# The last gate group in two halves: 256 columns in each of two banks

## The chip, the cores and the metric

The kernel runs on one core of one Trainium2 chip. The metric is the device time of one execution, in microseconds (us). TensorE multiplies and writes into PSUM, ScalarE (ACT) and VectorE (DVE) work on PSUM and SBUF, GpSimd (POOL) has no part in the end of this kernel, and SyncE (SP) issues the transfers.

## What is computed

One layer of a decoder trunk on x of 512 rows and 1024 columns, in float32: a mixer, a feed-forward part, and then the gate, followed by a last normalization. Only the last two matter here:

```python
h = h + (hid * hid) @ w_ff2[i]
gate = jax.nn.sigmoid(rmsnorm(h, ple_norm_g[i]) @ w_ple_gate[i])
h = h + gate * (p[i] @ w_ple_proj[i])
return rmsnorm(h, final_norm_g)
```

with rmsnorm(x, g) = x * rsqrt(mean(x * x) + 1e-6) * g, the mean taken over a row of 1024 columns.

## The kernel before

Every matrix product is done with operands that are split in two parts (a high part and the rest), both float32r: three matmuls of 512 columns stand for one product (`product`, lines 1120 to 1124: high by high, high by low, low by high). Rows go in four groups of 128 (s = 0 to 3). A block of weights b has 512 columns. PSUM has four banks `acc`, one for each row group, and four banks `side` for transposes.

The gate product comes last. It has two blocks, GATE and GATE + 1 (columns 0 to 511 and 512 to 1023), and so eight groups i = 0 to 7, with b = GATE + i // 4 and s = i % 4. For each, TensorE runs `group_rows` (line 1126): eight steps over k, each with the three matmuls of `product`, 24 matmuls of 512 columns into bank s of `acc`. The stationary operand is the normalized, transposed h (`b_hi`, `b_lo`), the moving one the weights (`w_hi`, `w_lo`). The last matmul of a group raises `acc_full`.

The order on each engine is written out by hand and strict. Engines meet only at semaphores. For each group ScalarE (lines 708 to 741) takes the sigmoid from the bank into `conv` (line 719), then in block GATE + 1 runs a square root of one column (line 722), whose only use is that the table of the square root is loaded at this point, then squares h with a row sum (line 727), and then: for a group of block GATE adds eps in an Identity (line 731, `f_base`), for a group of block GATE + 1 takes the square root over both halves of the row (line 735, `f_rms`). VectorE (lines 1075 to 1099) multiplies the gate into y, which holds p @ w_ple (line 1085, raises `gated`), adds it to h (line 1087, raises `h_final`, on which ScalarE's square waits), multiplies h by the gain of the last norm (line 1091, `h_gain`), and for block GATE + 1 takes the reciprocal (line 1094) and scales the whole row (line 1098). For the last group alone VectorE scales the first 640 columns and ScalarE the other 384 (line 740). SyncE sends each row group out as soon as it is scaled (line 355), and the program ends when the four transfers have landed.

A sigmoid and a square root are in different tables of ScalarE, so each group of block GATE + 1 has two ACT_TABLE_LOAD in the profile: one before its sigmoid (line 719), which runs as soon as the group before is finished, and one before the one-column square root (line 722). Square, Identity and Copy run with either.

Of the kernel before, what the change touches and what calls it, by code (L numbers as in the profile page):

```python
# [5 lines left out]
P = 128  # L6
F32 = mybir.dt.float32
F32R = mybir.dt.float32r
ALU = mybir.AluOpType
ACT = mybir.ActivationFunctionType  # L10
# [4 lines left out]
V, X, BC, U, Z, OUT, PLE, FF, GATE = 0, 2, 4, 5, 7, 9, 13, 14, 30  # L15
EPS = 1e-6
WARM = 10
OUT_DVE = 640


def build_layer(nc, a, out):


    _, SEQ, D = a["x"].shape
    NS = SEQ // P
    KT = D // P
# [22 lines left out]
    with ExitStack() as ctx:  # L49
        def sb(name, shape, dt=F32, where=ctx):  # L50
            return where.enter_context(nc.sbuf_tensor(name, shape, dt))
# [6 lines left out]
        w_hi = sb("w_hi", [P, 2, 8, 512], F32R)  # L58
        w_lo = sb("w_lo", [P, 2, 8, 512], F32R)
        a_hi = sb("a_hi", [P, KT, SEQ], F32R)  # L60
        a_lo = sb("a_lo", [P, KT, SEQ], F32R)
        h = sb("h", [P, NS, D])
        y = sb("y", [P, NS, D])
# [8 lines left out]
        cols = sb("cols", [P, 68])  # L72
# [7 lines left out]
        cs = sb("cs", [P, NS * R])  # L80
        csT = sb("csT", [NS * R, P])
        decay = sb("decay", [P, 3, NS, R])
        f_ssq = sb("f_ssq", [P, 8])
        f_base = sb("f_base", [P, NS])
        f_rms = sb("f_rms", [P, NS])
        f_rstd = sb("f_rstd", [P, NS])
        ssq = sb("ssq", [P, 12])
# [9 lines left out]
        with ExitStack() as early:  # L97
            conv = sb("conv", [P, 2, 512], where=early)
            xs_t = sb("xs_t", [P, 2, 512], where=early)
# [19 lines left out]
        b_hi = sb("b_hi", [P, KT, SEQ], F32R)  # L119
        b_lo = sb("b_lo", [P, KT, SEQ], F32R)  # L120


        acc = ctx.enter_context(nc.psum_tensor("acc", [P, 4, 512], F32))
# [8 lines left out]
        acc_full = sem("acc_full")  # L132
        act_evac = sem("act_evac")
# [34 lines left out]
        gated, h_final, h_gain = sem("gated"), sem("h_final"), sem("h_gain")  # L168
        f_ssq_ready, f_base_ready, f_rms_ready = sem("f_ssq_ready"), sem("f_base_ready"), sem("f_rms_ready")
# [21 lines left out]
        def emptied(b, s, shift=0):  # L191


            return (act_evac if kind[b].endswith("act") else dve_evac), before[b] + s + 1 + shift
# [228 lines left out]
        def _(act):  # L423
# [105 lines left out]
            for t in range(4 * OUT):  # L529
                b, s = divmod(t, 4)  # L530
# [14 lines left out]
                if 10 <= t < 18:  # L545
                    bank = wait_full(act, ("xs", t - 10))
                    if t == 10:
                        wait_free(act, ("ws", 1))
                    ins = act.activation(y[:, :, (t - 10) * P:(t - 10) * P + P],
                                         bank.rearrange("p (c n) -> p c n", c=NS), ACT.Copy)  # L550
                    freed(ins, ("xs", t - 10))
                if t == 11:
                    bank = wait_full(act, "dt")
                    act.wait_ge(small_landed, 16 * 4)
                    ins = act.activation(dtT[:], bank[0:2 * R, :], ACT.Identity, bias=dt_b[:])
# [5 lines left out]
                if t == 16:  # L561
                    bank = wait_full(act, "decay")
                    act.wait_ge(cs_ready, 1)
                    ins = act.activation(decay[:].rearrange("p a c r -> p (a c r)"), bank[:, 0:3 * NS * R], ACT.Exp)
                    freed(ins, "decay")
                if 16 <= t < 20:
                    for i in range(2):
                        head = 2 * (t - 16) + i
                        bank = wait_full(act, ("mix", head))
# [3 lines left out]
                if 19 <= t < 21:  # L573
                    g = t - 19
                    bank = wait_full(act, ("b_nat", g))
                    ins = act.activation(b_nat[:, g].rearrange("p c n -> p (c n)"), bank, ACT.Copy)
# [128 lines left out]
                sums(2, s)  # L705


            for i in range(8):
                b, s = GATE + i // 4, i % 4
                if i == 0:  # L710
                    xt_evac(2, 2)
                if i == 2:
                    xt_evac(2, 3)
                if b == GATE:
                    split_hi(GATE + 1, s)
                act.wait_ge(acc_full, 4 * b + s + 1)
                if i >= 2:
                    act.wait_ge(gated, i - 1)
                act.activation(conv[:, i % 2, :], acc[:, s, :], ACT.Sigmoid).then_inc(act_evac, 1)
                if b > GATE:  # L720
                    act.wait_ge(sqrt_loaded, s + 1)
                    act.activation(early_rms[:], eps[:], ACT.Sqrt).then_inc(sqrt_loaded, 1)

                act.wait_ge(h_final, i + 1)
                if i:
                    act.wait_ge(f_ssq_ready, i)
                act.activation(xs_t[:, 0, :], h[:, s, 512 * (i // 4):512 * (i // 4) + 512], ACT.Square,
                               accum_out=f_ssq[:, i:i + 1]).then_inc(f_ssq_ready, 1)
                act.wait_ge(f_ssq_ready, i + 1)
                if b == GATE:  # L730
                    act.activation(f_base[:, s:s + 1], f_ssq[:, i:i + 1], ACT.Identity, bias=eps[:], scale=1.0 / D
                                   ).then_inc(f_base_ready, 1)
                else:
                    act.wait_ge(f_base_ready, s + 1)
                    act.activation(f_rms[:, s:s + 1], f_ssq[:, i:i + 1], ACT.Sqrt, bias=f_base[:, s:s + 1],
                                   scale=1.0 / D).then_inc(f_rms_ready, 1)
                if i == 7:
                    act.wait_ge(f_rstd_ready, s + 1)
                    act.wait_ge(h_gain, 4 + s + 1)
                    act.activation(y[:, s, OUT_DVE:], y[:, s, OUT_DVE:], ACT.Copy, scale=f_rstd[:, s:s + 1]  # L740
                                   ).then_inc(out_act, 1)

# [2 lines left out]
        def _(dve):  # L745
# [326 lines left out]
                normed(2, s)  # L1072


            for i in range(8):
                b, s = GATE + i // 4, i % 4
                if i == 0:
                    xt_evac(2, 2)
                if i == 2:
                    xt_evac(2, 3)  # L1080
                if b == GATE:
                    split_lo(GATE + 1, s)
                at = slice(512 * (i // 4), 512 * (i // 4) + 512)
                dve.wait_ge(*emptied(b, s))
                dve.tensor_tensor(y[:, s, at], y[:, s, at], conv[:, i % 2, :], ALU.mult).then_inc(gated, 1)
                dve.wait_ge(gated, i + 1)
                dve.tensor_tensor(h[:, s, at], h[:, s, at], y[:, s, at], ALU.add).then_inc(h_final, 1)
                dve.wait_ge(h_final, i + 1)
                if i == 0:
                    dve.wait_ge(gain_landed[0], 16 * 4)  # L1090
                dve.tensor_tensor(y[:, s, at], h[:, s, at], gain[:, 0, at], ALU.mult).then_inc(h_gain, 1)
                if b > GATE:
                    dve.wait_ge(f_rms_ready, s + 1)
                    dve.reciprocal(f_rstd[:, s:s + 1], f_rms[:, s:s + 1]).then_inc(f_rstd_ready, 1)
                    dve.wait_ge(f_rstd_ready, s + 1)
                    dve.wait_ge(h_gain, i + 1)
                    end = OUT_DVE if i == 7 else D
                    dve.tensor_scalar(y[:, s, 0:end], y[:, s, 0:end], f_rstd[:, s:s + 1], None, ALU.mult
                                      ).then_inc(out_dve, 1)

# [2 lines left out]
        def _(pe):  # L1103
            def banks_free(b, s, trip=None):

                if b == 0:
                    return
                c, r = last_user(b, s)
                signal, value = emptied(c, r)
                pe.wait_ge(signal, value if trip is None else value + 8 * trip)  # L1110
                if trip is not None and b == FF + 1:


                    signal, value = emptied(FF + 4, 2 + s // 2)
                    pe.wait_ge(signal, value - 8 + 8 * trip)
# [4 lines left out]
            def product(dst, st, mv, start, stop):  # L1120

                pe.matmul(dst, st[0], mv[0], start=start, stop=False)  # L1122
                pe.matmul(dst, st[0], mv[1], start=False, stop=False)  # L1123
                return pe.matmul(dst, st[1], mv[0], start=False, stop=stop)  # L1124

            def group_rows(b, s, act_hl, between=None):


                banks_free(b, s)
                for k in range(KT):  # L1130
                    if between and k == KT - 2:
                        between()
                    if b == 0 and k % 4 == 0:
                        wait_free(pe, ("xt", 0, s, k // 4))
                    if s == 0 and k % 2 == 0:
                        split_ready(b, k // 2)
                    at = (slice(None), k, slice(s * P, s * P + P))
                    ins = product(acc[:, s, :], [t[at] for t in act_hl],
                                  [t[:, b % 2, k, :] for t in (w_hi, w_lo)], k == 0, k == KT - 1)
                ins.then_inc(acc_full, 1)  # L1140

            def group_cols(b, s, act_hl, trip=None):
# [215 lines left out]
            for i in range(8):  # L1358
                b, s = GATE + i // 4, i % 4
                if b == GATE:  # L1360
                    for q in range(2):
                        wait_free(pe, ("xt", 2, s, q))
                group_rows(b, s, B)
                if i == 1:
                    turn_norm(2, 3)

# [22 lines left out]
```

## Time and profile before

| | |
|---|---|
| time, median of 3 runs | 778.98 us (777.57, 778.98, 779.05) |
| span of the profiled execution | 775.9 us |
| time of the profiled execution | not recorded apart from its span |
| median less span | 3.1 us |
| TensorE busy | 763.0 us, 98% of the span |
| VectorE busy | 436.4 us, 56% |
| ScalarE busy | 326.1 us, 42% |
| mean granted clock of TensorE | 0.997 |

The span runs from the first to the last instruction of one execution; the time is that of executions without the profiler. A busy engine isn't an engine at its peak. The chain of work that ended last is followed back from the last instruction to what released each step. In a row of the timeline the columns are start, duration, engine, line, operation, tiles and shapes (partitions x elements), and in brackets how long the engine sat idle before and what ended this. "PE" is TensorE's matmul and "PEld" its loading of weights. The end of a matmul is modelled, and so the distance between the starts of two matmuls says more than their duration.

### The profile page before, as it was taken

Reading aid. Unit: us, or ns where it says so; the run is one execution under the profiler, and the core shown is the slowest. Engines: PE = TensorE matmul, PEld = TensorE weight load, DVE = VectorE, ACT = ScalarE, POOL = GpSimd, SP = SyncE. Lnnn points to the kernel's source line nnn. Section 1 sums busy time; section 2 is a strip of 40 time slices with the busy share of each in tenths; the row PEclk is TensorE's granted clock in tenths of the full one; section 3 lists DMA queues with packets and bytes.
Section 4 is the critical chain, followed back from the end, with each engine's and each line's share of the span. In section 5 each row is a group of like instructions: output and inputs, shape, how many; then the busy total and the mean of one; then the engine's idle time right before and its main releaser. Section 6 shows DMA issues by size and latency. Waiting matters only on the chain.

```text
span 775.9 us, 9090 instructions
## 1 busy us (share of the span) xinstructions
PE 763.0 (98%) x3492; PEld 623.3 (80%) x3492; DVE 436.4 (56%) x488; ACT 326.1 (42%) x456; POOL 87.5 (11%) x60
## 2 busy tenths in 40 slices
PE   8999999999999999999999999999999999999996
PEld 7888877888887888888888888888888888888885
DVE  5556884668579575457445353444444444446754
ACT  6525446655485823127433140413223140323556
POOL 1022210864652000000000000000000000000000
PEclk9999999999999999999999999999999999999998
DMA  8622333333323443123323233232323233232102
GB/s 333 187 82 82 108 98 115 116 108 103 143 82 103 166 139 110 44 76 124 109 85 106 87 103 108 81 108 81 108 81 108 81 102 97 92 122 82 48 0 109
DMA packets 35193, 81.88 MB, mean 106 GB/s; under 512 B 3924, under 2 KB 5592, under 8 KB 35160
## 3 DMA queue, kind: packets, MB, share of 16 engines
q1 hardware_dynamic: 33928, 77.20, 30.5%
q10 hardware_dynamic: 1232, 4.23, 1.8%
q8 instruction: 22, 0.36, 0.2%
q14 instruction: 11, 0.09, 0.0%
HBM read 79.28 MB, written 2.13 MB: 105 GB/s over the span
## 4 chain that ended last, share of the span: by engine, by line
PE 93%; DVE 3%; ACT 1%; issue 1%; DMA 1%; SPq 0%; ACTq 0%; DVEq 0%
PE acc L1122 29%; PE acc L1124 29%; PE acc L1123 29%; PE side L1184 3%; PE side L1277 2%; DVE w_lo L751 1%; PE side L1244 1%; DVE conv L948 1%; DMA gain<-in_norm_mix_g 1%; PE side L1284 1%; PE side L1272 1%; DVE h L937 0%; PE acc L1201 0%; ACT w_hi L431 0%; PE side L1224 0%
## 5 line engine op out<-in xcount | busy, mean ns | idle before, releaser
L1122 PE MATMUL acc<-w_hi,a_hi 128*128 128x512 f32 x512 | 204.2, 399 | 0.0
L1124 PE MATMUL acc<-w_hi,a_lo 128*128 128x512 f32 x512 | 199.5, 390 | 0.0
L1123 PE MATMUL acc<-w_lo,a_hi 128*128 128x512 f32 x512 | 199.4, 390 | 0.0
L431 ACT ACTIVATE w_hi<-w_raw 128x1024 fp32r<-128x1024 f32 (+1 forms) x128 | 130.1, 1036 | 145.9 <-PE acc L1124 143.6
L751 DVE TENSOR_TENSOR w_lo<-w_raw,w_hi 128x1024 fp32r<-128x1024 f32 (+1 forms) x128 | 166.1, 1299 | 45.0 <-ACT w_hi L431 44.3
L802 DVE TENSOR_TENSOR h<-h,acc 128x1024 f32<-128x1024 f32 x48 | 58.6, 1221 | 106.5 <-PE acc L1124 106.5
L1122 PEld LDWEIGHTS acc<-w_hi,a_hi 128*128 128x128 f32 x512 | 96.2, 188 | 21.0 <-issue 1.4
L1123 PEld LDWEIGHTS acc<-w_lo,a_hi 128*128 128x128 f32 x512 | 96.2, 188 | 20.6 <-issue 1.4
L1124 PEld LDWEIGHTS acc<-w_hi,a_lo 128*128 128x128 f32 x512 | 96.1, 188 | 20.3
L1124 PE MATMUL acc<-b_hi,w_lo 128*128 128x512 f32 x256 | 100.9, 394 | 0.0
L1122 PE MATMUL acc<-b_hi,w_hi 128*128 128x512 f32 x256 | 100.9, 394 | 0.0
L1123 PE MATMUL acc<-b_lo,w_hi 128*128 128x512 f32 x256 | 100.9, 394 | 0.0
L1048 DVE TENSOR_TENSOR tmp<-tmp 128x512 f32<-128x512 f32 x32 | 22.2, 693 | 76.5 <-ACT tmp L487 76.5
L487 ACT ACTIVATE tmp<-acc 128x512 f32<-128x512 f32 x32 | 19.1, 598 | 96.8 <-PE acc L1124 96.8
L1122 PEld LDWEIGHTS acc<-b_hi,w_hi 128*128 128x128 f32 x256 | 47.9, 187 | 11.9
L1124 PEld LDWEIGHTS acc<-b_hi,w_lo 128*128 128x128 f32 x256 | 47.9, 187 | 11.8
L1123 PEld LDWEIGHTS acc<-b_lo,w_hi 128*128 128x128 f32 x256 | 47.9, 187 | 11.8
L1122 PE MATMUL acc<-w_hi,b_hi 128*128 128x512 f32 x128 | 50.8, 397 | 0.0
L1124 PE MATMUL acc<-w_hi,b_lo 128*128 128x512 f32 x128 | 50.2, 392 | 0.0
L1123 PE MATMUL acc<-w_lo,b_hi 128*128 128x512 f32 x128 | 49.8, 389 | 0.0
L1122 PE MATMUL acc<-a_hi,w_hi 128*128 128x512 f32 x96 | 38.9, 405 | 0.0
L1124 PE MATMUL acc<-a_hi,w_lo 128*128 128x512 f32 x96 | 37.5, 390 | 0.0
(183 smaller groups left out, 819.1 us busy)
## 6 DMA issues: line engine op xcount, KB each, us to landing
w_raw<-in_w_ff SPq DMA_DIRECT2D x64, 512.0 KB, 3.5
w_raw<-in_w_in SPq DMA_DIRECT2D x36, 512.0 KB, 3.9
w_raw<-in_w_out SPq DMA_DIRECT2D x16, 512.0 KB, 3.4
h<-in_x SPq DMA_DIRECT2D x8, 512.0 KB, 4.4
seg<-cs_dram ACTq DMA_DIRECT2D x8, 512.0 KB, 3.8
w_raw<-in_w_ple_gate SPq DMA_DIRECT2D x8, 512.0 KB, 3.9
out<-y SPq DMA_DIRECT2D x4, 512.0 KB, 2.6
w_raw<-in_w_ple_proj SPq DMA_DIRECT2D x4, 256.0 KB, 2.6
```

The source lines that it names most:

```text
L431: act.activation(w_hi[:, half, 2 * p:2 * p + n, :], w_raw[:, p, 0:n, :], ACT.Copy).then_inc(hi_ready, 1)
L487: act.activation(tmp[:, s % 2, :], acc[:, s, :], ACT.Relu).then_inc(act_evac, 1)
L751: dve.tensor_tensor(w_lo[:, half, 2 * p:2 * p + n, :], w_raw[:, p, 0:n, :], w_hi[:, half, 2 * p:2 * p + n, :].bitcast(F32), ALU.subtract). ...
L802: dve.tensor_tensor(hs, hs, acc[:, i:i + 2, :], ALU.add).then_inc(dve_evac, 1)
L948: ins = dve.scalar_tensor_tensor(dst, acc[:, s, 0:SEQ - k], w, dst, ALU.mult, ALU.add)
L1048: dve.tensor_tensor(tmp[:, 2 + s % 2, :], tmp[:, s % 2, :], tmp[:, s % 2, :], ALU.mult).then_inc(sq_ready, 1)
L1122: pe.matmul(dst, st[0], mv[0], start=start, stop=False)
L1123: pe.matmul(dst, st[0], mv[1], start=False, stop=False)
L1124: return pe.matmul(dst, st[1], mv[0], start=False, stop=stop)
L1184: ins = pe.transpose(bank[:, i * P:i * P + P], src(i), ident[:])
L1244: filled(pe.matmul(bank.rearrange("p (c n) -> p c n", c=NS), wsT[:, g, :], h[:, :, g * P:g * P + P], start=True, stop=True), ("mix", g))
L1277: ins = pe.matmul(bank[:, r * HD:r * HD + HD], lm[:, r, :], xdt[:, r * HD:r * HD + HD], start=True, stop=True)
```

## The change

The eighth group (i = 7) becomes two, i = 7 and i = 8, with 256 columns each: 512 to 767 of the row into bank 3, 768 to 1023 into bank 0. TensorE runs eight steps over k for the first half and then eight for the second, with the same stationary tiles loaded again, so 48 matmuls of 256 columns. Before the second half it waits for the sigmoid of group 4 (i = 4), the last user of bank 0. ScalarE and VectorE do the steps of the two groups one after the other, in the same strict order, each step over 256 columns. The first half has no one-column square root; in place of the square root an Identity adds its sum of squares to `f_base` (a fifth column), and the second half's square root takes this as its bias. The reciprocal and the scaling come once, after the second half. `f_ssq` grows from 8 to 9 columns and `f_base` from 4 to 5. `emptied` is no longer asked for each group; the count that it gave for the first is counted up by i, which is the same number for i = 0 to 7.

```diff
@@ the tiles
-        f_ssq = sb("f_ssq", [P, 8])
-        f_base = sb("f_base", [P, NS])
+        f_ssq = sb("f_ssq", [P, 9])
+        f_base = sb("f_base", [P, NS + 1])
@@ ScalarE
-            for i in range(8):
-                b, s = GATE + i // 4, i % 4
+            for i in range(9):
+                b, s = (GATE + i // 4, i % 4) if i < 8 else (GATE + 1, 3)
...
-                act.wait_ge(acc_full, 4 * b + s + 1)
+                bank, n = (s, 512) if i < 7 else ((3, 256) if i == 7 else (0, 256))
+                at = slice(512 * (i // 4), 512 * (i // 4) + 512) if i < 7 else slice(512 + 256 * (i - 7), 768 + 256 * (i - 7))
+                act.wait_ge(acc_full, 4 * GATE + i + 1)
                 if i >= 2:
                     act.wait_ge(gated, i - 1)
-                act.activation(conv[:, i % 2, :], acc[:, s, :], ACT.Sigmoid).then_inc(act_evac, 1)
-                if b > GATE:
+                act.activation(conv[:, i % 2, 0:n], acc[:, bank, 0:n], ACT.Sigmoid).then_inc(act_evac, 1)
+                if b > GATE and i != 7:
                     act.wait_ge(sqrt_loaded, s + 1)
                     act.activation(early_rms[:], eps[:], ACT.Sqrt).then_inc(sqrt_loaded, 1)
 
                 act.wait_ge(h_final, i + 1)
                 if i:
                     act.wait_ge(f_ssq_ready, i)
-                act.activation(xs_t[:, 0, :], h[:, s, 512 * (i // 4):512 * (i // 4) + 512], ACT.Square,
+                act.activation(xs_t[:, 0, 0:n], h[:, s, at], ACT.Square,
                                accum_out=f_ssq[:, i:i + 1]).then_inc(f_ssq_ready, 1)
                 act.wait_ge(f_ssq_ready, i + 1)
                 if b == GATE:
                     act.activation(f_base[:, s:s + 1], f_ssq[:, i:i + 1], ACT.Identity, bias=eps[:], scale=1.0 / D
                                    ).then_inc(f_base_ready, 1)
+                elif i == 7:
+                    act.wait_ge(f_base_ready, s + 1)
+                    act.activation(f_base[:, 4:5], f_ssq[:, i:i + 1], ACT.Identity, bias=f_base[:, s:s + 1],
+                                   scale=1.0 / D).then_inc(f_base_ready, 1)
                 else:
-                    act.wait_ge(f_base_ready, s + 1)
-                    act.activation(f_rms[:, s:s + 1], f_ssq[:, i:i + 1], ACT.Sqrt, bias=f_base[:, s:s + 1],
+                    base = s if i < 7 else 4
+                    act.wait_ge(f_base_ready, base + 1)
+                    act.activation(f_rms[:, s:s + 1], f_ssq[:, i:i + 1], ACT.Sqrt, bias=f_base[:, base:base + 1],
                                    scale=1.0 / D).then_inc(f_rms_ready, 1)
-                if i == 7:
+                if i == 8:
                     act.wait_ge(f_rstd_ready, s + 1)
-                    act.wait_ge(h_gain, 4 + s + 1)
+                    act.wait_ge(h_gain, 9)
@@ VectorE
-                dve.wait_ge(*emptied(b, s))
-                dve.tensor_tensor(y[:, s, at], y[:, s, at], conv[:, i % 2, :], ALU.mult).then_inc(gated, 1)
+                dve.wait_ge(act_evac, emptied(GATE, 0)[1] + i)
+                dve.tensor_tensor(y[:, s, at], y[:, s, at], conv[:, i % 2, 0:n], ALU.mult).then_inc(gated, 1)
...
-                if b > GATE:
+                if b > GATE and i != 7:
                     dve.wait_ge(f_rms_ready, s + 1)
...
-                    end = OUT_DVE if i == 7 else D
+                    end = OUT_DVE if i == 8 else D
@@ TensorE
+            def last_half(half):
+
+                b, s, bank = GATE + 1, 3, (3, 0)[half]
+                if half == 0:
+                    banks_free(b, s)
+                else:
+                    pe.wait_ge(act_evac, emptied(b, 0)[1])
+                cols = slice(256 * half, 256 * half + 256)
+                for k in range(KT):
+                    ins = product(acc[:, bank, 0:256], [t[:, k, s * P:s * P + P] for t in (b_hi, b_lo)],
+                                  [t[:, b % 2, k, cols] for t in (w_hi, w_lo)], k == 0, k == KT - 1)
+                ins.then_inc(acc_full, 1)
...
-                group_rows(b, s, B)
+                if i < 7:
+                    group_rows(b, s, B)
+                else:
+                    for half in range(2):
+                        last_half(half)
```

## Rows read from the trace of the kernel before

**Rows 1.** The page: TensorE's share, and the chain's shares by engine.

```profile
PE 763.0 (98%) x3492; PEld 623.3 (80%) x3492; DVE 436.4 (56%) x488; ACT 326.1 (42%) x456; POOL 87.5 (11%) x60
...
PE 93%; DVE 3%; ACT 1%; issue 1%; DMA 1%; SPq 0%; ACTq 0%; DVEq 0%
```

**Rows 2.** The chain that ended last, from 765 us: start, duration, what.

```profile
768.57 0.25 PE acc L1124
...
769.45 1.28 ACT L722
```

**Rows 3.** Timeline of ScalarE, end of group 6 to the end.

```profile
766.49 1.28 ACT L719 ACT_TABLE_LOAD   x1
768.84 0.60 ACT L719 ACTIVATE conv<-acc 128x512 f32<-128x512 f32 x1 [1.06 <-PE acc L1124]
769.45 1.28 ACT L722 ACT_TABLE_LOAD   x1
770.75 0.20 ACT L722 ACTIVATE early_rms<-eps 128x1 f32<-128x1 f32 x1
770.92 0.63 ACT L727 ACTIVATE xs_t<-h 128x512 f32<-128x512 f32 x1
...
771.67 0.29 ACT L735 ACTIVATE f_rms<-f_ssq,f_base 128x1 f32<-128x1 f32 x1
772.20 0.61 ACT L740 ACTIVATE y<-y,f_rstd 128x384 f32<-128x384 f32 x1 [0.23 <-DVE f_rstd L1094]
```

**Rows 4.** Timeline of VectorE over the same stretch.

```profile
766.71 0.75 DVE L1098 TENSOR_SCALAR y<-y,f_rstd 128x1024 f32<-128x1024 f32 x1
769.47 0.69 DVE L1085 TENSOR_TENSOR y<-y,conv 128x512 f32<-128x512 f32 x1 [2.01 <-ACT conv L719]
770.19 0.69 DVE L1087 TENSOR_TENSOR h<-h,y 128x512 f32<-128x512 f32 x1
...
772.00 0.16 DVE L1094 RECIPROCAL f_rstd<-f_rms 128x1 f32<-128x1 f32 x1 [0.39 <-ACT f_rms L735]
```

**Rows 5.** Last group: first and last matmul, a load, the stretch with its granted clock.

```profile
763.14 0.39 PE L1122 MATMUL acc<-w_hi,b_hi 128*128 128x512 f32 x1
...
768.40 0.40 PE L1124 MATMUL acc<-w_hi,b_lo 128*128 128x512 f32 x1
...
763.14 0.19 PEld L1123 LDWEIGHTS acc<-w_lo,b_hi 128*128 128x128 f32 x1
...
763.14:768.60 5.46, 5.46 (x25) 4.32 (x23) 2.99 (x5) 4.36 (x7) 0.00 (x0) 1.00 0.24 97
```

**Rows 6.** Matmuls of 64 and 128 columns: durations (min/median/max), timeline, granted clock (1.00).

```profile
L1277 PEld LDWEIGHTS side<-xdt,lm x128: 187/192/192, 147.6 to 251.9; 128*128 128x128 f32 x128
L1277 PE MATMUL side<-xdt,lm x128: 218/275/275, 147.9 to 252.0; 128*128 128x64 f32 x128
...
147.87 1.89 PE L1277 MATMUL side<-xdt,lm 128*128 128x64 f32 x16
...
8.82 2.40 PE L1201 MATMUL acc<-ones,ident 128*128 128x128 f32 x20
...
147.87:149.54 1.67, 1.67 (x17) 1.67 (x15) 0.39 (x1) 1.67 (x3) 0.00 (x0) 1.00 0.26 49
```

**Rows 7.** Groups of instructions by form, 724 to 776 us, of 1024 columns.

```profile
L451 ACT ACTIVATE tmp<-h 128x1024 f32<-128x1024 f32 x1 | 1.1, 1059 | 3.1 <-DVE h L802 3.1
...
L751 DVE TENSOR_TENSOR w_lo<-w_raw,w_hi 128x1024 fp32r<-128x1024 f32 x4 | 4.9, 1222 | 2.8 <-ACT w_hi L431 2.7
```

**Rows 8.** Timeline of ScalarE, end of group 0.

```profile
732.33 0.29 ACT L731 ACTIVATE f_base<-f_ssq,eps 128x1 f32<-128x1 f32 x1
732.53 1.04 ACT L431 ACTIVATE w_hi<-w_raw 128x1024 fp32r<-128x1024 f32 x1
```

**Rows 9.** Output transfers: issues with first and last start, and landing times.

```profile
L355 SPq DMA_DIRECT2D out<-y x4: 332/344/356, 756.5 to 772.9; - x4
...
DMA to landing us min/median/max: 2.6/2.6/4.7
```

More of the change, by code:

```diff
@@ L1072, in _ @@
                 normed(2, s)
-            for i in range(8):
-                b, s = GATE + i // 4, i % 4
+            for i in range(9):
+                b, s = (GATE + i // 4, i % 4) if i < 8 else (GATE + 1, 3)
                 if i == 0:
@@ L1082, in _ @@
                     split_lo(GATE + 1, s)
-                at = slice(512 * (i // 4), 512 * (i // 4) + 512)
-                dve.wait_ge(*emptied(b, s))
-                dve.tensor_tensor(y[:, s, at], y[:, s, at], conv[:, i % 2, :], ALU.mult).then_inc(gated, 1)
+                n = 512 if i < 7 else 256
+                at = slice(512 * (i // 4), 512 * (i // 4) + 512) if i < 7 else slice(512 + 256 * (i - 7), 768 + 256 * (i - 7))
+                dve.wait_ge(act_evac, emptied(GATE, 0)[1] + i)
+                dve.tensor_tensor(y[:, s, at], y[:, s, at], conv[:, i % 2, 0:n], ALU.mult).then_inc(gated, 1)
                 dve.wait_ge(gated, i + 1)
```

## Prediction, made before the changed kernel was run

> **What bounds the kernel now.** I read three things in this order. First the busy shares and the chain's shares by engine [rows 1]: TensorE has work for 98% of the span and 93% of the chain that ended last runs through it. So for nearly all of the kernel a change has to touch TensorE's stream to be felt. Second, the end of that chain [rows 2]: it leaves TensorE with the last matmul at 768.57 us and goes on through ScalarE and VectorE. The change lives here, because its subject is the last group of matmuls, 128 rows by 512 columns of the gate product, and what must follow it before the output can be sent. Third, the tail instruction by instruction on ScalarE and VectorE [rows 3, 4]. From the start of the last sigmoid (768.84) to the start of the last output scaling (772.20) lie 3.36 us, and two chains run side by side in it:
> - ScalarE: sigmoid, 0.61 to the load of the square root's table, 1.30 to a one-column square root that only carries this load, 0.17 to the square [rows 3]. Sum 2.08.
> - VectorE: 0.63 to the gating product, 0.725 to the add into h and 0.725 until the square may start at 770.92 [rows 3, 4]. Sum 2.08.
>
> They end together. Behind them come square, read of its sum and square root (0.75 from 770.92 to 771.67), reciprocal (0.33), scaling (0.20 to its start) [rows 3, 4]. The output transfer is issued at 772.9 and lands 2.6 us later [rows 9]. The time before is 778.98 and the profiled span 775.9 (the table above), so 3.1 us lie around the span; the profiled execution has no separate time, and I take span plus 3.1 as its time, which is the median of the three runs by construction. The sum below gives a difference at 772.20, which goes unchanged into the span and the median, for the last transfer is the same size.
>
> **TensorE's part.** Removed are 24 matmuls of 512 columns, added are 48 of 256, each with its own load of 128x128 weights. The last group's matmuls start at 763.14 and 768.40, 23 intervals apart, so 0.2287 us each [rows 5]. The trace has no matmul of 256 columns. Bounds for its interval d:
> - The moving stream: half of 0.2287 is 0.114. At the upper of the two clock levels, 2.4 GHz, 512 columns take 0.213, so each matmul has 0.015 on top of its stream; 256 columns are then 0.107 + 0.015 = 0.122. The granted clock in this stretch is 1.00 [rows 5].
> - The weight load: sixteen matmuls of 64 columns, each with a load, take 1.89 us with the last one's own record of 0.275 taken off, so (1.89 - 0.275) / 15 = 0.108; twenty of 128 columns give (2.40 - 0.275) / 19 = 0.112 [rows 6]. A row of loads alone can't go faster than about 0.108, and it doesn't matter there whether 64 or 128 columns stream beside it. So load and stream lie beside each other.
> - Upper end: load and stream one behind the other, 0.108 + 0.114 = 0.222.
>
> I take 0.122, as the nearest rows (128 columns at 0.112 and 512 at 0.229, load hidden in both) lie on either side. The last matmul then starts at 763.14 + 47 x 0.122 = 768.87, 0.47 later than now. From its start to the sigmoid it is 0.44 now [rows 3, 5]; with 256 columns fewer in it 0.44 - 0.11 = 0.33. The second half is ready at 769.20 instead of 768.84. The first half is ready at 763.14 + 23 x 0.122 + 0.33 = 766.28. The second half's own wait, for bank 0, is for a sigmoid that ended over 10 us before, and costs nothing.
>
> **The 256-wide operations.** The trace has none of this width. ScalarE's square takes 1.059 us for 1024 and 0.63 for 512 columns [rows 3, 7], so 0.83 ns a column, and 256 columns fewer save 0.21. VectorE takes 1.222 for 1024 and 0.69 for 512 [rows 4, 7], 1.04 ns a column, and saves 0.265. Bounds: nothing is saved at all (ScalarE's scaling of only 384 columns took 0.61 [rows 3], no less than a sigmoid of 512), or the whole duration is halved. I take the slopes, since they come from the same engine and the same shapes of operand.
>
> **The first half.** The diff leaves ScalarE's program in strict order: sigmoid of the first half, its square, an Identity in place of the square root, and only then the sigmoid of the second half. The wait for h_final is new in this place: behind it on ScalarE stands the second sigmoid, and everything waits for that. When does the first sigmoid start? Not with its data (766.28): ScalarE finishes group 6 at 766.49 and then loads the sigmoid's table, as now, 1.30 to the next instruction [rows 3]. So it starts at 767.79. Then, each step now minus the saving:
> - sigmoid to product 0.63 - 0.21 = 0.42: 768.21
> - product to add 0.725 - 0.265 = 0.46: 768.67
> - add to square 0.46: 769.13
> - square and read to Identity 0.75 - 0.21 = 0.54: 769.67
> - Identity to the next instruction 0.20, by the Identity of group 0 at 732.33, followed at 732.53 [rows 8]: 769.87.
>
> No table load follows the Identity there, nor stands anywhere between the sigmoids of groups 0 to 3, so square and Identity run with the sigmoid's table. The multiply by the gain on VectorE ends at about 769.55 and is in nobody's way. VectorE had group 6's scaling from 766.71, 0.75 long [rows 4], so it is free at 767.46. The first half needs no table of the square root, and the second sigmoid follows with the table in place; so the number of loads is what it was, and one of them still stands behind the last sigmoid.
>
> So the second sigmoid starts at 769.87: its data are there at 769.20, and ScalarE is late by 0.67. TensorE's extra 0.47 is hidden under this, up to d = (769.87 - 0.33 - 763.14) / 47 = 0.136.
>
> **The second half.** Sigmoid to table load 0.61 - 0.21 = 0.40, table load 1.30, one-column square root 0.17, sum 1.87: the square starts at 771.74. VectorE's side needs only 0.42 + 0.46 + 0.46 = 1.34 and is hidden behind the table load, so the savings on the product and the add are worth nothing: what is late next is the table load, which the change doesn't shorten. Then 0.54, 0.33 and 0.20: the scaling starts at 772.81. The tail from the last sigmoid is 2.94 instead of 3.36, 0.42 shorter, but that sigmoid comes 1.03 later. The sum: 772.81 - 772.20 = +0.61. The scaling itself, its two waits and the transfer are the same.
>
> **Ends of the range.** With nothing saved by the smaller width: 767.79 + 0.63 + 0.73 + 0.73 + 0.75 + 0.20 = 770.83, and 3.36 behind it is 774.19, +1.99. With durations fully halved: 767.79 + 0.33 + 0.385 + 0.385 + 0.43 + 0.20 = 769.52, tail 2.74, 772.26, +0.06. The forecast is 778.98 + 0.61 = **779.6 us**. What a measurement of this kernel can tell from no change is about 0.2%, 1.56 us; so this counts as no change.
>
> **Rivals.**
> - *Load and stream don't overlap at 256 columns* (slower). Place: every matmul of the last group. For: the load's record is 0.19 us long [rows 5, 6], longer than a stream of 0.107. Against: the load-bound rows [rows 6] start one each 0.108, although the record is as long there. Price with d = 0.222: the last matmul starts at 773.57, the sigmoid at 773.90, the scaling at 776.84, +4.64: 783.6 us. It decides from d = 0.136, and is over 0.2% from d = 0.156 (sigmoid at 770.82). By the Trainium skill, "TensorE: Matmul & The Clock Gate", Part 3, a weight load overlaps matmuls in flight only where they use another row group of the array; here all use all rows, so by that rule it would come out this way. The trace disagrees with it already at 512 columns, where loads start each 0.23 us with the matmuls [rows 5]. Chance 3%.
> - *The clock falls with the short matmuls* (slower). At the lower level, 1.2 GHz, 256 columns take 0.213 + 0.015 = 0.228, the last starts at 773.86, and the same steps give about +4.9: 783.9 us. Against: TensorE isn't idle anywhere between the matmuls, and the 64-column stretch has a granted clock of 1.00 [rows 6]. [...] Chance 2%.
> - *Small widths cost as much as large ones*: +2.0, 781.0 us, slower by 0.26%, from the place worked out above. For it speaks the 384-column row, against it the slopes. Chance 3%.
> - *The change does what it is named for*, so that ScalarE isn't in the second half's way and the sigmoid starts when TensorE is done, at 769.20, or at 768.85 with d = 0.114. The scaling is then at 772.14 or 771.79: -0.06 to -0.41, 778.6 to 778.9 us. Against it is the table load at 766.49, which isn't touched [rows 3]. Chance 4%.
> - *Placement*: f_ssq and f_base grow, so all tensors declared after them move by some bytes, b_hi and b_lo among them. 1152 matmuls read these; 1.35 ns in each would be 1.56 us. Nothing in the trace bears on it. Chance 5%, either way.
>
> **How the numbers follow.** The forecast's case has 83%, of which a measurement may put 2 to faster and 1 to slower. Faster by over 0.2%: 2 + 2 of placement = 4%. Slower: 1 + 2 + 3 + 3 + 2 = 11%. Within: 80 + 4 + 1 = 85%. The range takes in the forecast's own bounds, +0.06 to +1.99, and at the lower end -0.4 of the rival and as much for where a median of runs falls that spread from 777.57 to 779.05: 778.2 to 781.3. The two rivals at 783 to 784 are left out.
>
> **What would show it.** In the profile after: matmuls of 256 columns some 0.12 us apart; the first half's sigmoid straight behind a table load, about 4.7 us behind the group's first matmul; the second half's sigmoid behind the Identity and not behind the last matmul, with an idle time of nearly nothing before it; the square behind the table load, with VectorE's add done 0.5 before. I'm wrong if the second sigmoid waits for TensorE (then d is over 0.136), or if the stretch ahead of the last group differs in length.

## The result, and the profile after

The changed kernel takes **781.65 us** (six runs, 781.49 to 781.82), the kernel before beside it 779.01 us (six runs, 777.57 to 780.41). The ratio is 1.0038, with a 95% interval of 1.0028 to 1.0049. It is slower by 0.38%, 2.6 us. The forecast was 779.6, no change, in a range of 778.2 to 781.3, with 11% for slower by over 0.2%.

The tail of the changed kernel, ScalarE's timeline from the end of group 6 (compare [rows 3]):

```profile
770.16 1.28 ACT L721 ACT_TABLE_LOAD   x1
771.45 0.39 ACT L721 ACTIVATE conv<-acc 128x256 f32<-128x256 f32 x1
772.78 0.42 ACT L729 ACTIVATE xs_t<-h 128x256 f32<-128x256 f32 x1 [0.95 <-DVE h L1095]
...
773.33 0.29 ACT L737 ACTIVATE f_base<-f_ssq,f_base 128x1 f32<-128x1 f32 x1
773.53 0.36 ACT L721 ACTIVATE conv<-acc 128x256 f32<-128x256 f32 x1
773.91 1.28 ACT L724 ACT_TABLE_LOAD   x1
775.20 0.20 ACT L724 ACTIVATE early_rms<-eps 128x1 f32<-128x1 f32 x1
775.31 0.40 ACT L729 ACTIVATE xs_t<-h 128x256 f32<-128x256 f32 x1
...
776.36 0.61 ACT L747 ACTIVATE y<-y,f_rstd 128x384 f32<-128x384 f32 x1 [0.23 <-DVE f_rstd L1102]
```

TensorE's timeline, the last matmul of 512 columns, then the first and last of the 48 of 256 (compare [rows 5]):

```profile
766.58 0.39 PE L1132 MATMUL acc<-w_hi,b_lo 128*128 128x512 f32 x1
766.81 0.28 PE L1130 MATMUL acc<-w_hi,b_hi 128*128 128x256 f32 x1
...
772.29 0.28 PE L1132 MATMUL acc<-w_hi,b_lo 128*128 128x256 f32 x1
```

From the last group's first matmul to the start of the last scaling: 776.36 - 766.81 = 9.55 us, against 772.20 - 763.14 = 9.06 before. So the tail accounts for +0.49, much as worked out (+0.61). But the last group begins 3.67 us later than before (766.81 against 763.14), in a part of the program that the change does not edit. I paired every matmul of one trace with the same matmul of the other. The lag, by which a matmul starts later than its partner before, grows in four places:

| where (time of before) | lag at its start and end | growth, us | what runs there |
|---|---|---|---|
| the start, to 37 us | 0 to 1.53 | +1.53 | TensorE at another clock, see below |
| mixer, 130 to 264 us | 1.57 to 1.91 | +0.35 | matmuls of several kinds |
| second half of the output product, and p @ w_ple, 304 to 369 us | 1.91 to 2.91 | +1.00 | matmuls with b or p stationary |
| gate product, 724 us to its last group | 2.96 to 3.67 | +0.7 | matmuls with b stationary |

In the feed-forward part, 354 us long, the lag stays as it is (2.91 to 2.96). Here and below, w stands for the weights (`w_hi`, `w_lo`), a and b for the two tensors of transposed activations (`a_hi`, `a_lo`, `b_hi`, `b_lo`), p for `p_hi`, `p_lo`. The operand that a weight load brings in is stationary, the other one moving. In the gate product b is stationary and w moving; in the feed-forward part there are 768 matmuls with w stationary and b moving.

The first place has nothing to do with the edit. TensorE's timeline there, of before and then of after, and the view by stretch, 9 to 12 us, of before and then of after (columns: length, busy TensorE with its count, loads, VectorE, ScalarE, GpSimd, granted clock, DMA share, GB/s):

```profile
7.89 1.09 PE L1184 MATMUL side<-ident,h 128*128 128x128 f32 x8 [1.52 <-DVE h L767]
```

```profile
7.99 1.09 PE L1205 MATMUL side<-ident,h 128*128 128x128 f32 x8 [1.94 <-DVE h L774]
```

```profile
9.00:12.00 3.00, 3.00 (x25) 2.82 (x25) 3.00 (x4) 2.81 (x5) 0.00 (x0) 1.00 1.04 408
```

```profile
9.00:12.00 3.00, 3.00 (x16) 3.00 (x15) 3.00 (x4) 2.91 (x5) 0.00 (x0) 0.50 1.04 398
```

In the profiled execution of after TensorE is at 1.2 GHz there, after it sat idle for 1.94 us, until 7.99, for the first normalized rows; in that of before it is at 2.4 GHz, after 1.52 us idle. Executions of one and the same kernel fall into groups some 1.4 us apart: in 23 runs of the kernel before, ten lie at 777.56 to 777.82 and thirteen at 778.70 to 779.22 (single ones elsewhere lie 1.4 higher still, 780.41 above and 780.55 on another chip). The clock goes with the group. The profiled executions of after, e3, e4 and e7 have 0.50 in this row and, where their kernel's runs show both groups, are of the slower one; those of before, e1, e8, e10, e11 and e12 have 1.00 and are of the faster one. The other four (e2, e5, e6, e9) lie between in the spacing of their matmuls. So the span of 775.9 belongs to an execution of 777.6 and not to the median: 1.7 us lie around a span, not 3.1. All six runs of after lie within 0.33 us of each other, and the profiled one has the slower start. Below I compare kernels by distances within their traces, and by medians where these are further apart than 1.4 us.

Without the start, the traces differ by 4.16 - 1.53 = 2.63 us, which is the measured 2.64: 2.1 before the last group and 0.5 behind it.

### The profile page after: what moved, and what is told of

Read it like the earlier page. It is cut to its first block, busy times and chain, and to the rows that moved or that the text cites. A ratio compares the mean times of both kernels' runs of the same rounds, so it can differ in the third digit from the quotient of the medians.

```text
span 780.1 us, 9148 instructions
## 1 busy us (share of the span) xinstructions
PE 766.5 (98%) x3516; PEld 626.6 (80%) x3516; DVE 436.6 (56%) x491; ACT 326.8 (42%) x460; POOL 87.4 (11%) x60
## 4 chain that ended last, share of the span: by engine, by line
PE 93%; DVE 3%; ACT 2%; issue 1%; DMA 1%; SPq 0%; ACTq 0%; DVEq 0%
PE acc L1130 28%; PE acc L1132 28%; PE acc L1131 28%; PE side L1205 3%; PE side L1298 2%; DVE w_lo L758 1%; PE side L1265 1%; DVE conv L955 1%; DMA gain<-in_norm_mix_g 1%; PE side L1305 1%; PE side L1293 1%; PE acc L1222 0%; DVE h L944 0%; ACT L724 0%; ACT w_hi L431 0%
## 5 line engine op out<-in xcount | busy, mean ns | idle before, releaser
L1130 PE MATMUL acc<-w_hi,b_hi 128*128 128x512 f32 (+1 forms) x136 | 52.4, 385 | 0.0
L1131 PE MATMUL acc<-w_lo,b_hi 128*128 128x512 f32 (+1 forms) x136 | 51.9, 382 | 0.0
L1132 PE MATMUL acc<-w_hi,b_lo 128*128 128x512 f32 (+1 forms) x136 | 51.8, 381 | 0.0
```

## The experiments

**What moved the 2.1 us.** TensorE's operands lie elsewhere in SBUF. The change grows `f_ssq` from 8 to 9 columns. The program lays tensors out in the order of their declarations, each in a multiple of 32 bytes in each partition. 36 bytes take 64 instead of 32, so every tensor declared behind it starts 32 bytes later (`f_base` with 20 bytes still fits in 32). Adding up the declarations, `b_hi` starts 162,240 bytes behind `w_hi` before, which is 192 behind a multiple of 256, and 224 behind one after; `p_hi`, `p_lo` and `b_lo` have the same remainder as `b_hi`, and `a_hi` and `a_lo` have remainder 0. All distances below are such sums; no trace shows an address. Where an expectation says that a tensor starts at or behind a multiple of 256, this holds counted from w; where w itself starts isn't known from any run.

*e1_place*: the growth alone.

```diff
-        f_ssq = sb("f_ssq", [P, 8])
-        f_base = sb("f_base", [P, NS])
+        f_ssq = sb("f_ssq", [P, 9])
+        f_base = sb("f_base", [P, NS + 1])
```

> The kernel before with one edit: f_ssq is declared with 9 columns and f_base with 5, and the added columns are never used. Nothing is computed otherwise; all tensors declared behind them start 32 bytes later. Placement theory: the 240 matmuls over b and p before the feed-forward part and the 192 gate matmuls, all with these tensors stationary, come 0.2335 us apart instead of 0.229, some +1.9 us, and the mixer stage adds up to 0.4: 781.0 to 781.4 us, slower by 0.25 to 0.3%. Rival (the rest of the measured +2.6 comes from the halves themselves or from the start): no difference to before, 779.0 us, intervals 0.229.

Measured: 781.08 us against 778.78, ratio 1.0030 (1.0019 to 1.0042). This profile has the same faster start as the profile of before. The interval is taken over 143 gate matmuls of 512 columns, as the distance between the first and the last over 142. The first one in before (the last is the 768.40 of [rows 5]), then the first and last in e1_place:

```profile
735.89 0.40 PE L1123 MATMUL acc<-w_lo,b_hi 128*128 128x512 f32 x1
```

```profile
737.42 0.39 PE L1123 MATMUL acc<-w_lo,b_hi 128*128 128x512 f32 x1
...
770.55 0.39 PE L1124 MATMUL acc<-w_hi,b_lo 128*128 128x512 f32 x1
```

32.51 / 142 = 0.2289 us, and 33.13 / 142 = 0.2333 us: 4.4 ns more in each. The lag grows in the same places and by the same amounts as in after (0.33 in the mixer, 1.00 to 369 us, 0.69 in the gate product up to 763 us). Two declarations, with not one instruction changed, give four fifths of the result: +2.04 us at the last group's first matmul, with the same start.

*e2_halves*: the halves alone.

```diff
-        f_ssq = sb("f_ssq", [P, 9])
+        f_ssq = sb("f_ssq", [P, 8])
...
         b_lo = sb("b_lo", [P, KT, SEQ], F32R)
+        f_ssq8 = sb("f_ssq8", [P, 1])
```

with `f_ssq8` in place of the ninth column in the two instructions that use it.

> The changed kernel, with the ninth sum of squares in a tensor of its own that is declared behind all others, so that every other tensor starts where it did before the change. Placement theory: intervals of the gate matmuls of 512 columns back at 0.229 us, those of 256 columns at 0.115 to 0.117, and only the tail is longer, by the 0.5 to 0.6 us of the prediction's steps: 779.5 us, within 0.2% of before. Rival: the halves cost more than the tail shows, 781.6 us as the changed kernel.

Measured: 778.43 us against 778.78, ratio 1.0002 (0.9993 to 1.0011). The medians differ by -0.35 only because more of these runs had the faster start; group by group it is 778.2 against 777.6 and 779.6 against 779.0, +0.6. In the trace the lag to before is 1.39 at 130 us and 1.39 at the last group, so nothing grows, and the tail takes 774.09 - 764.53 = 9.56 us, +0.50:

```profile
764.53 0.28 PE L1131 MATMUL acc<-w_hi,b_hi 128*128 128x256 f32 x1
...
774.09 0.62 ACT L748 ACTIVATE y<-y,f_rstd 128x384 f32<-128x384 f32 x1 [0.23 <-DVE f_rstd L1103]
```

This is what the prediction described.

**Is it a multiple, and of what?** Even before the change b was not placed well. In [rows 5] the last group's matmuls have 0.2287 us; with a as the stationary operand a row of 96 has 0.2268. In five kernels (e3, e4, e6, e11, e12) an unused tensor was put ahead of `conv`:

```diff
         m_rstd = sb("m_rstd", [P, 12])
+        pad = sb("pad", [P, 16])
```

with 16, 32, 48, 24 and 80 columns (64, 128, 192, 96 and 320 bytes). All five move `conv`, `xs_t`, p and b together, against w, a, h and y.

> The kernel before with an unused tensor of 64 bytes a partition ahead of conv, so that p, b and the mixer's tensors start at a multiple of 128 bytes (256 too) as a and w do, instead of 64 bytes behind one. Placement theory in its strong form (128 bytes matter as well): stationary b goes from 0.229 to 0.2275 us and moving b, 768 matmuls of the feed-forward part, from 0.2333 to 0.2275: 774 us, -0.65%. Weak form (only the step of 32 within 64 bytes matters): as before, 779.0 us, and the 0.2333 of the moving b has another cause.

> The same with 128 bytes, so that these tensors again start 64 bytes behind a multiple of 128, but 64 instead of 192 behind a multiple of 256. If the place within 64 or 128 bytes is what counts: as before, 779.0 us, with 0.229 and 0.2333. If the distance from the other tensors, or the place within 256 bytes, counts: another time than both the kernel before and the 64-byte one.

> The kernel before with 192 unused bytes ahead of conv: p and b start 128 bytes behind a multiple of 256. If the place within 128 bytes is what counts: 0.2266 and 0.2270 us as in the 64-byte run, 772.9 us. If the place within 256 bytes counts: intervals between those of the 64-byte and the 128-byte run or above, 774 to 779 us.

> The kernel before with 96 unused bytes ahead of conv: p and b start 32 bytes behind a multiple of 256. If being off a multiple of 64 by 32 costs the stationary side what it did in the change: stationary b at 0.2333 us, moving b between 0.2266 and 0.2333; 777 to 781 us.

> The kernel before with 320 unused bytes ahead of conv: the distance from w to b is again a multiple of 256 bytes, but no longer one of 512, as it is in the 64-byte run and between w and a. If a distance of a multiple of 256 is enough: moving b 0.2266 and stationary b 0.2270 us, 772.9 us. If it has to be 512: intervals above that, 774 to 779 us.

*e7_all64* puts 64 unused bytes ahead of all tensors instead, so that w and a move as well and every distance between tensors stays.

```diff
+        pad = sb("pad", [P, 16])
         w_raw = sb("w_raw", [P, 4, 2, 512])
```

> The kernel before with 64 unused bytes ahead of the very first tensor: w and a now start 64 bytes behind a multiple of 256, p and b at a multiple. If each operand's own place counts: the matmuls of w with a, some 1700 of them, which had 0.2275 us, get 0.230 to 0.234, +4 to +11 us, those with b moving too since w is out of place, so slower than before by 0.5 to 1.5%. If the distance between the two operands counts: w with a stays at 0.2275 and w with b at 0.2333 and 0.229, 779.0 us.

The intervals of matmuls of 512 columns, in ns, each from the first and the last of a row of 96 to 192 that follow one another (119 to 143 for stationary b); each ratio is to runs of before on the same chip:

| kernel | b behind w, in bytes modulo 256 | stationary b | moving b | time, us | ratio to before |
|---|---|---|---|---|---|
| before | 192 | 228.9 | 233.3 | 779.0 | 1 |
| changed | 224 | 233.3 | 233.4 | 781.65 | 1.0038 (1.0028 to 1.0049) |
| e1_place | 224 | 233.3 | 233.4 | 781.08 | 1.0030 (1.0019 to 1.0042) |
| e7_all64 | 192 | 228.9 | 233.3 | 779.05 | 1.0003 (0.9993 to 1.0014) |
| e11_pad96 | 32 | 233.3 | 233.4 | 779.93 | 1.0029 (1.0017 to 1.0040) |
| e4_pad128 | 64 | 233.4 | 233.4, later 229.1 | 777.72 | 0.9995 (0.9986 to 1.0004) |
| e6_pad192 | 128 | 232.3 | 233.4 | 779.63 | 1.0019 (1.0007 to 1.0030) |
| e3_pad64 | 0 | 227.0 | 226.6 | 772.87 | **0.9921** (0.9907 to 0.9934) |
| e12_pad320 | 0 (256 modulo 512) | 226.9 | 226.6 | 772.44 | **0.9926** (0.9910 to 0.9943) |

Where w and a meet, always with remainder 0, the feed-forward rows of 96 have 226.6 to 227.2. This too moves a little with b, which these matmuls don't read: 226.7 with b at remainder 0, 226.9 at 192 and 224, 227.0 at 32, 227.2 at 64. First and last of 192 feed-forward matmuls with moving b, in before and then in e3_pad64:

```profile
367.67 0.39 PE L1122 MATMUL acc<-b_hi,w_hi 128*128 128x512 f32 x1
...
412.23 0.39 PE L1124 MATMUL acc<-b_hi,w_lo 128*128 128x512 f32 x1
```

```profile
368.88 0.39 PE L1123 MATMUL acc<-b_hi,w_hi 128*128 128x512 f32 x1
...
412.17 0.39 PE L1125 MATMUL acc<-b_hi,w_lo 128*128 128x512 f32 x1
```

44.56 / 191 = 0.2333 and 43.29 / 191 = 0.2266. First and last of the 143 gate matmuls in e7_all64, 32.51 / 142 = 0.2289 as in before:

```profile
737.51 0.40 PE L1124 MATMUL acc<-w_lo,b_hi 128*128 128x512 f32 x1
...
770.02 0.40 PE L1125 MATMUL acc<-w_hi,b_lo 128*128 128x512 f32 x1
```

What follows:

- A distance of a multiple of 256 bytes between the two operands gives the short interval on both sides; 512 isn't needed (e12). All five other remainders tried give 228.9 to 233.4 ns on either side.
- It is a distance and not a place. In e7 every tensor starts 64 bytes further on, and nothing differs from before, w with a included; in e3, where w and a stay and b and p start 64 bytes further on, both intervals get shorter. My expectation by each operand's own place, +4 to +11 us, fell.
- That it is the distance between the two operands of a matmul is argued, not isolated. For it speaks that in one and the same trace matmuls with b and without it differ by up to 6.4 ns. But `conv` and `xs_t` move with b, and no run moves b alone.
- e3 was to be 774 us in the strong form and 779 in the weak one. It came out at 772.87: 768 matmuls with moving b by 6.7 ns and 432 with b or p stationary by 1.9 ns are 6.0 us, and 5.9 were measured.
- For e6 the form "the place within 128 bytes" expected 772.9; it was 779.63 and fell.
- With remainder 64 (e4) the moving b begins at 233.4 ns (192 matmuls from 370 us) and is at 229.1 in every later block of 96. The static distance is the same in all of them. So the distance of the two operands isn't the whole of it, and the runs don't show what else is.

**Does ScalarE's order delay the second half?** The remaining kernels have b at remainder 0, so they are measured against e3_pad64: 772.87 us, the last group's first matmul at 758.76 and the scaling at 767.76, 9.00 us between them.

*e5_halves_al*: the change with 32 more bytes ahead of `conv`.

```diff
+        pad = sb("pad", [P, 8])
```

> The changed kernel with an unused tensor of 32 bytes ahead of conv, so that p and b start at a multiple of 256 bytes as in the 64-byte run, with the change's own two halves. Placement theory: intervals of 0.2265 to 0.2275 throughout, and against the 64-byte run without the halves only the tail differs, by +0.5 us: 773.4 us, ratio to before 0.993. Rival (the halves have a price or a gain of their own besides the tail): off that by over 0.8 us either way.

Measured: 773.76 us, ratio 0.9936 (0.9922 to 0.9951), scaling at 768.33 - 758.78 = 9.55 us, +0.55 to e3. The halves cost the same at all three placements (0.49, 0.50, 0.55): half a microsecond in the tail is all that they do.

*e8_one_square*, with 64 bytes ahead of `conv` and `f_ssq` and `f_base` of their old sizes: ScalarE takes the second sigmoid directly after the first and squares all 512 columns at once.

```diff
+                if i == 7:
+                    continue
+                j = min(i, 7)
                 act.wait_ge(h_final, i + 1)
...
-                act.activation(xs_t[:, 0, 0:n], h[:, s, at], ACT.Square,
-                               accum_out=f_ssq[:, i:i + 1]).then_inc(f_ssq_ready, 1)
+                act.activation(xs_t[:, 0, :], h[:, s, 512 * (j // 4):512 * (j // 4) + 512], ACT.Square,
+                               accum_out=f_ssq[:, j:j + 1]).then_inc(f_ssq_ready, 1)
```

> The halves in another order on ScalarE, placed as the 64-byte run: no square and no Identity of the first half; the second sigmoid follows the first directly, and one square over all 512 columns follows the table load. Theory that ScalarE's own order delays the second sigmoid: it now starts when TensorE is done, 5.8 us behind the group's first matmul (before: 5.7, the change: 6.7), and from there to the scaling 0.38 + 1.29 + 0.11 + 0.75 + 0.33 + 0.20 = 3.06: 8.87 us behind the group's first matmul against 9.06 before and 9.55 in the change. 772.7 us, within noise of the 64-byte run. Rival (the second sigmoid is late because of TensorE or the bank): it starts 6.7 us behind as in the change.

Measured: 773.26 us, ratio 0.9929 (0.9915 to 0.9943). ScalarE's timeline; the group's first matmul is at 757.37, its last at 763.00:

```profile
762.01 0.39 ACT L722 ACTIVATE conv<-acc 128x256 f32<-128x256 f32 x1
763.32 0.38 ACT L722 ACTIVATE conv<-acc 128x256 f32<-128x256 f32 x1 [0.92 <-PE acc L1131]
763.72 1.28 ACT L725 ACT_TABLE_LOAD   x1
...
766.39 0.62 ACT L746 ACTIVATE y<-y,f_rstd 128x384 f32<-128x384 f32 x1 [0.23 <-DVE f_rstd L1101]
```

The second sigmoid now waits for TensorE and starts 5.95 us behind the first matmul, not 6.72, and 0.32 behind the last matmul's start (0.33 was the estimate). So in the change it was ScalarE's own order that held it: the first half's square and Identity stand between the two sigmoids. The scaling is at 9.02, equal to the 9.00 of e3: what the order gives back is just what the halves had cost. The 0.15 to the expected 8.87 is TensorE's: its interval at 256 columns is (763.00 - 757.37) / 47 = 0.1198 here, against 0.1166 in the change.

**What eats the gain?** *e9_identity* and *e10_id_halves* leave out the square root of the last norm in groups 4 and up, without the halves and with them, so that ScalarE needs no table load between the groups.

```diff
-                    act.activation(early_rms[:], eps[:], ACT.Sqrt).then_inc(sqrt_loaded, 1)
...
-                    act.activation(f_rms[:, s:s + 1], f_ssq[:, i:i + 1], ACT.Sqrt, bias=f_base[:, s:s + 1],
+                    act.activation(f_rms[:, s:s + 1], f_ssq[:, i:i + 1], ACT.Identity, bias=f_base[:, s:s + 1],
```

> The kernel before, placed as the 64-byte run, in which the last norm leaves out the square root: Identity instead, so no table load is needed from group 4 on, nor the one-column square root. Theory (without the load VectorE's chain, which is exactly as long, sets the same end): from the last sigmoid to the scaling still 3.36 us, 9.06 behind the group's first matmul, 772.9 us. Rival: the load alone held the end, and up to 1.3 us go.

> The halves of the change, placed as the 64-byte run, with the square root left out in the same way. Theory (the table load ate the halves' gain): the first sigmoid starts with its data, 3.1 us behind the group's first matmul, its square and Identity are done at 5.2, the second sigmoid starts at 5.8, and from there 0.42 + 0.46 + 0.46 + 0.54 + 0.33 + 0.20 = 2.41: the scaling at 8.2, 0.8 us earlier than without the halves, about 772.0 us. Rival (halving brings nothing on this chip even so, for instance because fixed costs of the steps or TensorE's interval eat it): scaling at 9.0 or later.

Measured: e9 772.94 us, ratio 0.9920 (0.9904 to 0.9935), scaling 767.81 - 758.81 = 9.00 behind the first matmul. Its square waits for VectorE now:

```profile
764.45 0.60 ACT L720 ACTIVATE conv<-acc 128x512 f32<-128x512 f32 x1 [2.31 <-PE acc L1122]
766.53 0.63 ACT L725 ACTIVATE xs_t<-h 128x512 f32<-128x512 f32 x1 [1.48 <-DVE h L1085]
```

e10 771.31 us, ratio 0.9908 (0.9891 to 0.9925), 765.87 - 757.51 = 8.36. ScalarE's timeline in e10:

```profile
760.76 0.36 ACT L722 ACTIVATE conv<-acc 128x256 f32<-128x256 f32 x1
762.66 0.42 ACT L727 ACTIVATE xs_t<-h 128x256 f32<-128x256 f32 x1 [1.54 <-DVE h L1093]
...
763.46 0.38 ACT L722 ACTIVATE conv<-acc 128x256 f32<-128x256 f32 x1
764.80 0.42 ACT L727 ACTIVATE xs_t<-h 128x256 f32<-128x256 f32 x1 [0.95 <-DVE h L1093]
...
765.87 0.62 ACT L745 ACTIVATE y<-y,f_rstd 128x384 f32<-128x384 f32 x1 [0.23 <-DVE f_rstd L1100]
```

Taking the table loads away alone gives nothing (9.00), since VectorE's chain is as long, 2.08 from the sigmoid to the square as in [rows 3]. The halves without the loads give 0.64 us; with them they cost 0.5. Expected were 0.8: the tail from the second sigmoid is 2.41 as worked out, but that sigmoid comes 5.95 behind the first matmul, not 5.8, because TensorE's interval is 0.120 (last matmul at 763.15). The first half's square is late, 1.90 behind its sigmoid and not 1.34, since VectorE was still at group 6's scaling, but it is done just in time and costs nothing. So the halves pay in a tail without a table load, and what they meet here is a load ahead of the first half and one behind the second.

## Why the prediction was wrong, point by point

- **The placement**, the last of its rivals, with 5%, is what happened. The sum of the forecast had it at nothing; it measured +2.1 of the 2.6 us, and e1, which changes nothing but the declarations, shows it. The prediction's own sign of being wrong, another length of the stretch ahead of the last group, is the one that came. Two steps failed there. "Nothing in the trace bears on it" is not so: the trace of before holds long rows of matmuls of one shape at 0.2269 us (w with a), 0.2289 (w moving, b stationary) and 0.2333 (b moving). I read only the last group's 0.2287 and didn't ask why equal matmuls differ. A spread of up to 6.4 ns between the tensors was the price, and 408 matmuls with stationary b or p ahead of the last group, times 4.4 ns, are 1.8 of the 2.1 us; the 768 with b moving didn't change (0.2333 and 0.2334). And having written the mechanism down with 1152 matmuls, I left its size at what the noise bound needed instead of at that spread.
- **The range** ends at 781.3, which is 0.3 above the +1.99 that it was to take in; the prediction doesn't say from what. It holds nothing for the placement.
- **The time around the span**, 3.1 us, was 1.7. The other 1.4 were between runs with the faster and the slower start. It didn't enter the difference, but it made the profiled execution look typical.
- **TensorE's interval** at 256 columns: estimated 0.122, measured 0.1166. That refutes the serial rival (0.222). With it falls, for this kernel, the rule of the Trainium skill cited there ("TensorE: Matmul & The Clock Gate", Part 3), that a load overlaps matmuls only in another row group. The clock's rival fell too: the 48 matmuls run evenly at this interval.
- **The widths**: sigmoid 0.36 to 0.39, VectorE's operations 0.42 to 0.43, square 0.40 to 0.42, as the slopes gave (0.39, 0.43, 0.42). The upper bound "a small width costs the same" was far too wide.
- **First half**: its sigmoid 4.64 behind the first matmul, straight behind the table load (estimated 4.65). **Second half**: its sigmoid at 6.72 (6.73), behind the Identity and with TensorE long done. From there to the scaling 2.83, not 2.94; the one-column square root is followed by the square after 0.11, not 0.17. The tail is +0.49 for the estimated +0.61, and e8 shows that the cause is the one named. This part of the mechanism was right.
- **"The change does what it is named for"**, the rival in which ScalarE isn't in the way, is refuted for this order; e8 makes it true and gains 0.5 to the change, and nothing to the kernel before.

Open is the mixer's +0.35 us: it goes with the placement (0.33 in e1, none in e2), but many tensors move there and no run separates them. In e3, where b is placed best, this stretch is also 0.2 slower.

## What to carry to other kernels

Before pricing an edit, compare the intervals of matmuls of one shape over different tensors: if they differ, placement has a price, and an edit that only adds a column to a small tensor can collect it over thousands of instructions. Here 64 unused bytes, which put the two operands of every large matmul a multiple of 256 bytes apart, bring 0.8%, more than twice what the change lost. Splitting the last group cost half a microsecond with the table loads and gained 0.64 us without them. So before splitting a group, ask what is late next: a step of fixed length, as a table load of 1.28 us, isn't halved.

## What the runs showed of the hardware

- In long rows of 512-column float32r matmuls the interval goes with the distance between stationary and moving operand modulo 256 bytes: 226.6 to 227.2 ns at 0, 228.9 to 233.4 at 32, 64, 128, 192 and 224. 128 isn't enough (232.3 and 233.4). At 64 the moving side changes between two values within one trace (233.4, then 229.1), which the distance doesn't explain.
- At 256 columns the order is the other way round: 119.8 ns at distance 0 (e5, e8, e10), 117.9 at 192 (e2), 116.6 at 224 (the change). From 116.6 to 119.8 costs the halved group 0.15 us; why, no run tells.
- After an idle time of 1.4 to 2.2 us before 8 us the clock is at 1.2 or 2.4 GHz from one execution to the next (granted 0.50 or 1.00 from 9 to 12 us), which is 1.4 us in the whole time. In the profile of e2 the first matmuls are as far apart as at the lower level (15 of them in 2.72 us) while the granted clock is recorded as 1.00, so the record alone didn't tell it there.
